# A two-layer trunk on one core: the first layer's experts in pairs with a side block, token lists by a product, the second filter spectrum moved

## The chip, the cores and the metric

One core of one Trainium2 chip runs the whole program. The metric is device time in microseconds, the median of the runs shown. All data and all arithmetic are float32. On TensorE every float32 product of this program stands in the trace as two MATMUL instructions and two weight loads, so "8 products" in the text are "x16" in a row.

## The reference, cut to what matters

Two layers work on 256 latent tokens and 256 context tokens, 1024 channels each. A layer has a part with four parallel token mixers and then a part with a mixture of experts. The second layer computes its last part for the latent tokens alone.

```python
def hier_moe(h, ...):                 # per token: best of 4 groups, then best 2 of that group's 4 experts
    gi = argmax(t @ w_rg + b_rg)      # group, weight gw = softmax at gi
    top_p, top_i = top_k(softmax(le[gi]), 2)
    ...
def expert_block(xblk, e):
    u = silu(xblk @ w1[e]) * (xblk @ w3[e])   # 1024 -> 512, twice
    return u @ w2[e]                          # 512 -> 1024
...
y = segment_sum(yb * buf_w[:, None], buf_tok) # each token gets its two weighted results
```

There are 16 experts. A token counts for two of them, so the first layer has 1024 assignments (64 per expert on average) and the second has 512 (32 on average). By the reference's own routing of these inputs the busiest expert has 86 assignments in the first layer (latent and context tokens together) and 48 in the second. One of the mixers (Hyena) convolves with a filter that a small network computes for each layer; the kernel brings it to the frequency domain with products (`fnorm`, `fdft`).

## The kernel before

**Order of the work.** `layer_order` writes one list of steps (engine, name) by hand, for TensorE (T), VectorE (V), ScalarE (S) and GpSimd (P). Each engine runs its own steps strictly in this order and waits on counting semaphores for the others. Steps of TensorE take the 8 PSUM banks in turn. On VectorE nearly every small instruction waits for the one before it (`link`). A second list (`CHUNKS`) sets the order in which SyncE's queue loads weights into a ring of three 2 MB places; a place is loaded again when its last reader has finished.

**Experts.** `xg` holds 128 gathered token rows; TensorE turns them (8 transposes, L1218 and L1125), VectorE and ScalarE copy them to `xgT`. Then come 8 products of 512 columns for the gate (`w1`), 8 for up (`w3`), 4 transposes of the hidden rows, and 4 + 4 products for down (`w2`). ScalarE and VectorE do the tanh form of silu between them, and ScalarE stores 128 result rows (512 KB) to `y_scratch`.
- First layer (not `paired`): 16 blocks of up to 128 rows, one expert each. Lines: gate L1229, up L1233, down L1249 and L1254, transposes L1218 and L1239. The weights of one expert are three 2 MB loads. The down products of expert e-1 stand behind gate and up of expert e.
- Second layer (`paired`): 8 blocks of two experts, 64 rows each. `both_halves` gives the even expert PSUM partitions 0 to 63 (L1130) and the odd one 64 to 127 (L1132), each with a stationary tile of 64 columns. The odd experts' weights lie in `n_` (w1), `hT` (w3) and `wide` (w2), so a pair takes six 2 MB loads: two behind each of gate, up and down of the pair before.
- If an expert has more assignments than its block has rows (`room`: 128, or 64 where paired), a branch runs more blocks, with every expert's weights loaded again.

**Routing.** From `lgout` (L2094) VectorE goes through route1 to route3 with two exponentials on ScalarE between them; ScalarE copies the transposed tokens (`hbout`, L1509) behind the second exponential and stores them to `h_scratch`. TensorE ranks the assignments (`rank`, L1104 to L1109), VectorE makes their places (`slots`), GpSimd scatters token numbers to a list in HBM (L1660; 8 DMAs in the first layer, 4 in the second), waits, reads the list back (L1665), copies an index and gathers the first block (L1674). While that goes on, VectorE runs the gate steps (`modgate`, L1832), and in the first layer TensorE, VectorE and ScalarE compute the second layer's filter spectrum (`fnorm` L930, `fnorms` L1925 to L1929, `fdft` L938 and L942, `fdftout` L1396 to L1403).

**Ahead of the routing** stands the last projection: 8 steps `wo` (L1076), their sums into `x` (L2086, L2088), squares (L1349), the scaled tokens `xn` (L1356 on ScalarE), and their transposes (`hT`, L878).

**Behind the experts** GpSimd waits for the last store of results and gathers each token's two rows (L1696, 8 DMAs in the first layer), ScalarE and VectorE weigh and add them, and the next layer begins.

## Time and profile before

| | |
|---|---|
| median of 3 runs (lowest to highest) | 1824.85 us (1823.38 to 1829.51) |
| profiled execution: its own time | 1827.23 us |
| its span in the trace | 1825.5 us |
| TensorE busy | 1553.3 us, 85% of the span |
| VectorE, ScalarE, GpSimd busy | 33%, 17%, 6% |
| mean TensorE clock granted | 0.924 of full speed |
| moved by DMA | 365.12 MB, mean 200 GB/s |
| first layer's experts, first gate product to last down product | 735.05 to 1100.06 us |
| second layer's experts, the same | 1558.19 to about 1802 us |

How to read it: the busy shares are averages over stages with different limits. The stage tables (busy time of each engine in a stretch, with clock and DMA rate) say what limits a stage; the timeline says which wait ends last in it. The clock column is the share of full speed; TensorE has two levels, 2.4 GHz (1.00) and 1.2 GHz.

### The profile page before, as it was taken

The page shows a single profiled execution, that of the slowest core. Times are in us where ns is not written, and L with a number is a line of the kernel's source. Part 1 is how long each engine was busy: PE and PEld are TensorE (multiplying, and loading weights), DVE is VectorE, ACT ScalarE, POOL GpSimd, SP SyncE. Part 2 cuts the span into 40 slices and gives each one's busy share as a digit, 9 for nine tenths or more (in the row PEclk, how much of TensorE's full clock was granted, in tenths as well). Part 3 has the DMA queues.
Part 4 walks back from the last instruction along what each step waited for, and adds up shares of the span by engine and source line. Part 5 has one row for each costly group of instructions (what it writes and reads, how often), then busy time and mean ns, then how long its engine had stood idle before and what let it go on. Part 6 is the DMA issues. An engine that isn't in the chain of part 4 may idle for free. (4 is left out here: it accounts for less than half of the span.)

```text
span 1825.5 us, 15949 instructions
## 1 busy us (share of the span) xinstructions
PE 1553.3 (85%) x5618; PEld 805.0 (44%) x5618; DVE 598.5 (33%) x1456; ACT 305.5 (17%) x611; POOL 115.6 (6%) x149
## 2 busy tenths in 40 slices
PE   5999998888999985999999982799979993887873
PEld 2444643433444444444444430655757862332321
DVE  4366443545432135111111102663555224010002
ACT  3112012221322112011111101211232201000000
POOL 0000000000111002000000001000001101000000
PEclk9999998999999997899999986899989996898997
DMA  9255021133111221588989857173212354799994
GB/s 381 108 231 218 35 92 69 47 138 116 46 67 53 92 92 50 225 329 335 337 333 338 331 193 311 46 283 131 94 74 111 116 220 172 281 431 426 428 427 190
DMA packets 34684, 365.12 MB, mean 200 GB/s; under 512 B 4256, under 2 KB 4656, under 8 KB 13888
## 3 DMA queue, kind: packets, MB, share of 16 engines
q1 hardware_dynamic: 24640, 329.67, 46.3%
q0 software_dynamic: 5664, 18.93, 2.7%
q10 hardware_dynamic: 4320, 15.73, 2.1%
q8 instruction: 36, 0.59, 0.1%
q14 instruction: 24, 0.20, 0.0%
HBM read 347.50 MB, written 16.82 MB: 200 GB/s over the span
## 5 line engine op out<-in xcount | busy, mean ns | idle before, releaser
L895 PE MATMUL ps<-hT,ring 128*128 128x512 f32 (+1 forms) x1344 | 460.5, 498 | 4.9 <-DVE hT L1858 3.2
L895 PEld LDWEIGHTS ps<-hT,ring 128*128 128x128 f32 x1344 | 258.7, 195 | 188.6 <-issue 160.8
L1130 PE MATMUL ps<-ring,m 128*64 128x512 f32 x384 | 186.8, 644 | 45.6 <-DMA n_<-w 19.7
L905 PE MATMUL ps<-ring,hT 128*128 128x512 f32 (+1 forms) x352 | 127.7, 522 | 2.5 <-DMA ring<-win 2.5
L1130 PEld LDWEIGHTS ps<-ring,m 128*64 128x64 f32 x384 | 54.9, 148 | 163.0 <-issue 140.7
L1229 PE MATMUL ps<-ring,m 128*128 128x512 f32 x256 | 115.5, 605 | 1.0 <-DVE m L2263 1.0
L1233 PE MATMUL ps<-ring,m 128*128 128x512 f32 x256 | 112.6, 593 | 0.3 <-DMA ring<-w 0.3
L993 PE MATMUL ps<-yT,ring 128*128 128x512 f32 (+1 forms) x256 | 94.5, 491 | 2.3 <-ACT n_ L1471 2.2
L905 PEld LDWEIGHTS ps<-ring,hT 128*128 128x128 f32 x352 | 67.0, 192 | 62.3 <-issue 58.1
L1076 PE MATMUL ps<-ring,wide 128*128 128x512 f32 x192 | 82.8, 593 | 0.8 <-POOL wide L1635 0.8
L1989 DVE SCALAR_TENSOR_TENSOR gtmp<-gth,ps 128x512 f32<-128x512 f32 (+1 forms) x48 | 26.6, 555 | 173.0 <-PE ps L993 149.5
L1430 ACT ACTIVATE gth<-ps,hbg 128x512 f32<-128x512 f32 (+1 forms) x64 | 37.1, 580 | 273.0 <-PE ps L895 212.7
L1233 PEld LDWEIGHTS ps<-ring,m 128*128 128x128 f32 x256 | 48.6, 190 | 61.9 <-issue 60.7
L1899 DVE SCALAR_TENSOR_TENSOR n_<-n_,col 128x512 f32<-128x512 f32 (+1 forms) x120 | 74.2, 618 | 4.3
L1229 PEld LDWEIGHTS ps<-ring,m 128*128 128x128 f32 x256 | 48.5, 194 | 56.9 <-issue 55.2
L1635 POOL TENSOR_TENSOR wide<-wide,gtmp 128x512 f32<-128x512 f32 (+1 forms) x48 | 47.9, 998 | 398.3 <-DVE gtmp L1989 398.3
L1132 PE MATMUL ps<-n_,m 128*64 128x512 f32 x128 | 69.2, 703 | 0.0
L1249 PE MATMUL ps<-ring,m 128*128 128x512 f32 x128 | 60.3, 616 | 8.2 <-issue 8.2
L2267 DVE SCALAR_TENSOR_TENSOR m<-m,ps 128x512 f32<-128x512 f32 x16 | 11.0, 687 | 166.6 <-ACT m L1575 166.6
L1132 PE MATMUL ps<-hT,m 128*64 128x512 f32 x128 | 61.6, 638 | 0.0
L854 PE MATMUL ps<-ring,cc 128*32 128x512 f32 x384 | 52.1, 665 | 10.7 <-DMA ring<-wmod 10.7
L1471 ACT ACTIVATE n_<-ps,nm 128x512 f32<-128x512 f32 (+1 forms) x72 | 43.9, 613 | 103.2 <-DVE nm L2031 56.0
(316 smaller groups left out, 1543.6 us busy)
## 6 DMA issues: line engine op xcount, KB each, us to landing
ring<-w SPq DMA_DIRECT2D x72, 2048.0 KB, 8.5
ring<-wmod SPq DMA_DIRECT2D x24, 2048.0 KB, 9.3
ring<-win SPq DMA_DIRECT2D x24, 2048.0 KB, 8.5
n_<-w SPq DMA_DIRECT2D x8, 2048.0 KB, 21.8
hT<-w SPq DMA_DIRECT2D x8, 2048.0 KB, 22.8
wide<-w SPq DMA_DIRECT2D x8, 2048.0 KB, 23.0
y_scratch<-m ACTq DMA_DIRECT2D x24, 512.0 KB, 8.5
ring<-wbr SPq DMA_DIRECT2D x8, 1024.0 KB, 4.8
```

What stands on the lines that cost most here:

```text
L854: last = pe.matmul(b[g:g + 32, :], cc[:, 32 * k:32 * k + 32], w[:, k, :], start=(k < 4), stop=(k >= 4), skip_group_check=True)
L895: last = pe.matmul(b[:, 0:W], w[:, k, jj * P:(jj + 1) * P], hT[:, k, 0:W], start=(k == 0), stop=(k == KD - 1))
L905: last = pe.matmul(b[:, 0:wid], hT[:, k, t * P:(t + 1) * P], w[:, k, 0:wid], start=(k == 0), stop=(k == KD - 1))
L993: last = pe.matmul(b[:, 0:W], w[:, k, j * P:(j + 1) * P], yT[:, bi in (1, 2), k, 0:W], start=(k == 0), stop=(k == 1))
L1076: last = pe.matmul(b, acc[:, k, t * P:(t + 1) * P], w[:, k, :], start=(k == 0), stop=(k == KD - 1))
L1130: pe.matmul(ps[0:HALF, bnk, :], left[:, k, 0:HALF], even[:, k, cols_], start=(k == 0), stop=(k == n_k - 1), skip_group_check=True)
L1132: last = pe.matmul(ps[HALF:P, bnk, :], left[:, k, HALF:P], odd[:, k, cols_], start=(k == 0), stop=(k == n_k - 1), skip_group_check=True)
L1229: last = pe.matmul(ps[:, 2, :], xgT[:, k, :], wg[:, k, :], start=(k == 0), stop=(k == KD - 1))
L1233: last = pe.matmul(ps[:, 3, :], xgT[:, k, :], wu[:, k, :], start=(k == 0), stop=(k == KD - 1))
L1249: last = pe.matmul(ps[:, 5, :], uT[:, f, :], wd[:, f, 0:512], start=(f == 0), stop=(f == 3))
L1635: last = nc.gpsimd.tensor_tensor(acc[:, j, 0:W], acc[:, j, 0:W], gtmp[:, g % 2, 0:W], ALU.add)
L1899: last = v.scalar_tensor_tensor(out=o, in0=ud[:, j, 0:ns, k:k + 256], scalar=w(k), in1=o, op0=ALU.mult, op1=ALU.add)
```

## The change

Three things, in all of both layers' routing and experts:

1. **Pairs in the first layer too, with a side block.** Every layer uses 8 blocks of two experts with 64 rows each. In the first layer (`with_side`) ranks 64 to 95 of each expert go to a side block: `side_x` has 64 rows, 32 for each expert of the pair. `four_quarters` runs products with stationary tiles of 32 columns on the four quarters of PSUM's partitions: for gate and up the quarters are (even, odd) by (lower, upper half of the 1024 channels), and VectorE adds the halves; for down they are (even, odd) by (lower, upper 512 outputs). A weight place is loaded again once the side block too has read it. `room` is 96 in the first layer and 64 in the second. TensorE's eight pairs are written out; the other engines write out the first and last pair and loop over the rest.
2. **Lists made on the chip.** The two exponentials go behind the list (`weights1`, `rexp`, `weights2`), `picks` holds the rest of the routing in fewer instructions. A product of one-hot ranks (`at_rank`) and token numbers (`token_of`) gives `lst` straight in PSUM; a second one gives the side block's list. The places of the results (`rows`) follow in VectorE's order, still ahead of its experts step. The scatter to HBM stays for the overflow branch alone. ScalarE copies the gates (`modgate`) of chunks 10 and 11.
3. **The second filter spectrum** moves from behind the routing to the last projection: `fnorm` and `fnorms` behind the first `wo` step, the four `fdft` behind the last, `fdftout` behind ScalarE's last square and ahead of its last `xn`.

```diff
 # layer_order
     for t in range(tt):
         for hf in range(2):
             o += [("T", ("wo", l, t, hf))]
+            if t == hf == 0 and spectrum:
+                o += spectrum[0]
...
             o += [("V", ("xup", l, t, hf))]
+    o += [g[0] for g in spectrum[1:]]
     o += [("S" if t % 2 else "V", ("xn", l, 2, t)) for t in range(tt - 1)]
-    o += norm_steps(l, 2, [tt - 1]) + modulated_steps(l, 2)
-    o += [("T", ("lg", l)), ("S", ("lgrow", l)), ("T", ("lgT", l)), ("V", ("lgout", l))]
-    o += [("V", ("route1", l)), ("S", ("rexp1", l)), ("V", ("route2", l)), ("S", ("rexp2", l)), ("V", ("route3", l))]
+    normed = norm_steps(l, 2, [tt - 1])
+    o += normed[:1] + [g[1] for g in spectrum[1:]] + normed[1:] + modulated_steps(l, 2)
+    o += [("T", ("lg", l)), ("S", ("lgrow", l)), ("T", ("lgT", l)), ("V", ("lgout", l)), ("V", ("picks", l))]
...
-    o += [("T", ("rank", l)), ("V", ("slots", l)), ("P", ("list", l))]
+    o += [("T", ("rank", l)), ("V", ("slots", l)), ("T", ("list", l)), ("V", ("list", l))]
+    if with_side(l):
+        o += [("V", ("sideslots", l)), ("T", ("sidelist", l)), ("V", ("sidelist", l))]
     o += gate_steps(l, (10, 11))
-    for g in spectrum:
-        o += g
+    o += [("V", ("weights1", l)), ("S", ("rexp", l)), ("V", ("weights2", l)), ("V", ("rows", l))]
     o += [("T", ("experts", l)), ("S", ("experts", l)), ("V", ("experts", l)), ("P", ("experts", l))]
 # SyncE, pairs 1 to 7
+                        for w in ("w1", "w3", "w2"):
+                            sp.wait_ge(last_reader(w, l), base + e)
+                            sp.dma_start(at[w][0], pairs_of[w][l, e, 0]).then_inc(at[w][1], 16)
+                            sp.dma_start(odd_at[w], pairs_of[w][l, e, 1]).then_inc(odd_landed[w], 16)
 # TensorE
+                elif kind == "list":
+                    for i, (q, t) in enumerate(choices):
+                        last = pe.matmul(b[:, 0:NE], at_rank[:, q * TILES + t, 0:P], token_of[:, q, t * NE:(t + 1) * NE],
+                                         start=(i == 0), stop=(i == len(choices) - 1))
...
+                    def four_quarters(bnk, left, quarters):
+                        for k in range(4):
+                            for g, (weights, k0, rows_, cols_) in enumerate(quarters):
+                                last = pe.matmul(ps[SIDE * g:SIDE * (g + 1), bnk, :], left[:, k0 + k, rows_:rows_ + SIDE],
+                                                 weights[:, k0 + k, cols_], start=(k == 0), stop=(k == 3),
+                                                 skip_group_check=True)
...
                     def gate_and_up(e):
...
                         both_halves(2, xgT, wg, wg2, slice(0, FE), KD).then_inc(gate_done, 1)
+                        if side:
+                            pe.wait_ge(side_xT_ready, e + 1)
...
+                            four_quarters(7, side_xT, split_k(wg, wg2)).then_inc(side_gate_done, 1)
                         both_halves(3, xgT, wu, wu2, slice(0, FE), KD).then_inc(up_done, 1)
+                        if side:
...
+                            four_quarters(6, side_xT, split_k(wu, wu2)).then_inc(side_up_done, 1)
...
+                    def pair(e, more):
+                        gate_and_up(e)
+                        if more:
+                            pe.wait_ge(tokens_gathered, e * 16 + 16 * (base + 2))
+                            turn_tokens()
+                        turn_u(e)
+                        if side and more:
+                            pe.wait_ge(side_gathered, e * 16 + 32)
+                            pe.wait_ge(side_gate_sum, e + 1)
+                            turn_side()
+                        down(e, more)
 # ScalarE, behind result(e)
+                        if side:
+                            act.wait_ge(side_y_ready, e + 1)
+                            act.dma_start(side_rows_of[e, :, 0:FE], side_y[0:HALF, :]).then_inc(side_y_stored, 16)
+                            act.dma_start(side_rows_of[e, :, FE:D], side_y[HALF:P, :]).then_inc(side_y_stored, 16)
 # GpSimd: no list step; the gathers take their index straight from lst
+                        gp.indirect_dma_start(out=xg, out_offset=None, in_=h2_dram,
+                                              in_offset=bass.IndirectOffsetOnAxis(ap=lst[:, e:e + 1], axis=0))\
+                          .then_inc(tokens_gathered, 16)
...
+                        gp.indirect_dma_start(out=side_x, out_offset=None, in_=h2_dram,
+                                              in_offset=bass.IndirectOffsetOnAxis(
+                                                  ap=lst[0:HALF, PAIRS + e:PAIRS + e + 1], axis=0))\
+                          .then_inc(side_gathered, 16)
 # VectorE
+                elif kind == "slots":
...
+                    link(v.tensor_scalar(ranks[:, 0:tt, :].rearrange("p t e -> p (t e)"), b[:, 0:tt * NE], 256.0, None, ALU.mult))
+                    link(v.tensor_tensor(pd, pk, ranks[:, 0:tt, :].unsqueeze(1).broadcast_to([P, 2, tt, NE]), ALU.mult))
+                    link(v.tensor_reduce(place_rank[:, :, 0:tt], pd, AX.X, ALU.add))
+                    last = one_hot_ranks(l, slice(0, P), 0, HALF)
```

In `down(e, more)` the side block's 4 transposes stand between the lower and the upper half, and its four quarters behind the upper half.

## Rows read from the trace of the kernel before

**Rows 1.** The page: its head, and a VectorE group (count, busy, mean ns).
```profile
span 1825.5 us, 15949 instructions
...
L1899 DVE SCALAR_TENSOR_TENSOR n_<-n_,col 128x512 f32<-128x512 f32 (+1 forms) x120 | 74.2, 618 | 4.3
```

**Rows 2.** Stages: first layer's experts; 32 us of the second's.
```profile
core 0: us, PE busy (x) PEld busy (x) DVE busy (x) ACT busy (x) POOL busy (x), PEclk, DMA share, GB/s
735.00:1100.00 365.00, 356.34 (x952) 166.56 (x952) 43.44 (x63) 37.02 (x62) 17.04 (x29) 0.98 0.81 302
...
1603.00:1635.00 32.00, 25.35 (x117) 9.78 (x115) 3.70 (x6) 3.30 (x6) 1.33 (x3) 0.95 1.00 427
```

**Rows 3.** Timeline, TensorE, first layer's experts: start us, us, what, count.
```profile
735.05 9.90 PE L1229 MATMUL ps<-ring,m 128*128 128x512 f32 x16 [0.85 <-DVE m L2263]
...
1060.93 7.03 PE L1229 MATMUL ps<-ring,m 128*128 128x512 f32 x16
...
1067.80 7.03 PE L1233 MATMUL ps<-ring,m 128*128 128x512 f32 x16
...
1096.46 3.60 PE L1254 MATMUL ps<-ring,m 128*128 128x512 f32 x8
```

**Rows 4.** Timeline, TensorE, second layer: a pair's last up products to its first down.
```profile
1573.62 0.59 PE L1130 MATMUL ps<-ring,m 128*64 128x512 f32 x1
1573.62 0.59 PE L1132 MATMUL ps<-hT,m 128*64 128x512 f32 x1
1574.05 0.59 PE L1130 MATMUL ps<-ring,m 128*64 128x512 f32 x1
...
1574.58 1.09 PE L1125 MATMUL ps<-con,m 128*128 128x128 f32 x8
...
1575.51 0.66 PE L1151 MATMUL ps<-con,m 128*128 128x128 f32 x4
...
1577.04 0.61 PE L1130 MATMUL ps<-ring,m 128*64 128x512 f32 x1 [0.87 <-ACT m L1543]
```

**Rows 5.** Timeline, TensorE: one modulation step, 8 products on four partition quarters.
```profile
1115.02 1.92 PE L854 MATMUL ps<-ring,cc 128*32 128x512 f32 x16
```

**Rows 6.** Timeline, first layer's routing, from lgout to the turned first block.
```profile
692.44 0.24 DVE L2094 TENSOR_TENSOR m<-m,row 128x80 f32<-128x80 f32 x1
...
703.10 0.69 PE L1104 MATMUL ps<-m,con 128*128 128x80 f32 x2 [7.80 <-DVE m L2151]
...
705.60 0.17 DVE L2192 CAST m<-con 128x4 uint32<-128x4 f32 x1 [2.64 <-PE ps L1109]
...
711.88 0.17 DVE L2213 CAST m<-m 128x16 uint32<-128x16 f32 x1
...
712.95 1.04 POOL L1660 DMA_INDIRECT list_scratch<-m  x1 [94.55 <-issue]
...
727.93 1.01 POOL L1674 DMA_INDIRECT m<-h_scratch,m  x1 [0.52 <-POOL m L1672]
...
732.26 1.94 PE L1218 MATMUL ps<-con,m 128*128 128x128 f32 x8 [6.25 <-DMA m<-h_scratch,m]
```

**Rows 7.** Timeline, second layer: end of lgout, and the first gate product.
```profile
1522.15 0.20 DVE L2094 TENSOR_TENSOR m<-m,row 128x40 f32<-128x40 f32 x1
...
1558.19 1.11 PE L1130 MATMUL ps<-ring,m 128*64 128x512 f32 x1 [1.11 <-DVE m L2221]
```

**Rows 8.** Timeline: the filter spectrum, and TensorE's wait behind the last projection.
```profile
680.75 1.52 PE L878 MATMUL ps<-con,wide 128*128 128x128 f32 x6 [6.78 <-ACT wide L1356]
...
708.70 3.41 PE L930 MATMUL ps<-con,m 128*128 128x1 f32 x16
...
724.38 0.38 ACT L1399 ACTIVATE m<-ps 128x256 f32<-128x256 f32 x1 [0.40 <-PE ps L938]
```

**Rows 9.** Timeline, end of the first layer: last store of results, first gather of them.
```profile
1100.72 0.35 ACTq L1586 DMA_DIRECT2D y_scratch<-m  x1
...
1114.10 0.94 POOL L1696 DMA_INDIRECT wide<-y_scratch,m  x1 [80.12 <-ACTq L1612]
```

More of the change, by code:

```diff
@@ L36 @@
 HALF = P // 2
+SIDE = HALF // 2
 FE = 512
@@ L430, in readers @@
            "yM": ("V", "yrA"), "yR": ("V", "ynA"), "yC": ("S", "yToutC"),
-           "wo": ("V", "xup"), "lg": ("S", "lgrow"), "lgT": ("V", "lgout"), "hb": ("S", "hbout"), "rank": ("V", "slots")}
+           "wo": ("V", "xup"), "lg": ("S", "lgrow"), "lgT": ("V", "lgout"), "hb": ("S", "hbout"), "rank": ("V", "list"),
+           "list": ("V", "list"), "sidelist": ("V", "sidelist")}
     if kind in one:
@@ L434, in readers @@
         return [(e, (k, l, *rest))]
+    if kind == "modB":
+        return [(spreader(rest[0]), ("modgate", l, *rest))]
     if kind == "yA":
@@ L1152, in turn_u, with turn_side_u, down @@
                         last.then_inc(u_turned, 1)
-                    def down(e):
+                    def turn_side_u(e):
+                        pe.wait_ge(side_u_ready, e + 1)
+                        for f in range(4):
+                            last = pe.transpose(ps[:, 2, f * HALF:(f + 1) * HALF], side_u[:, f * P:(f + 1) * P],
+                                                ident[0:HALF, 0:HALF])
+                        last.then_inc(side_u_turned, 1)
+                    def down(e, more):
@@ L1176, in _ @@
+                    for e in range(PAIRS):
+                        pair(e, e < PAIRS - 1)
                     pe.wait_ge(y_low, base + PAIRS)
                     pe.wait_ge(y_high, base + PAIRS)
+                    if side:
+                        pe.wait_ge(side_y_ready, PAIRS)
                     count = assignments(pe, l)
-                    with pe.If(count > HALF):
+                    with pe.If(count > room(l)):
                         with pe.Fori(0, more_blocks(l) * NE) as n_block:
@@ L1676, in _ @@
-                    with gp.Fori(1, blocks(l)) as e:
-                        gp.wait_ge(tokens_turned, base + e)
-                        gp.tensor_copy(idx1, lst[:, bass.ds(e, 1)]).then_inc(index_ready, 1)
-                        gp.wait_ge(index_ready, base + e + 1)
-                        gp.sem_inc(waited, 1)
+                    gp.wait_ge(vector_done, vector("list", l))
+                    for e in range(PAIRS):
+                        if e:
+                            gp.wait_ge(tokens_turned, base + e)
@@ L2153, in _ @@
                     last.then_inc(vector_done, 1)
-                elif kind == "slots" and paired(l):
+                elif kind == "slots":
+                    pk = pick[:, :, 0:tt * NE].rearrange("p q (t e) -> p q t e", e=NE)
+                    for q in range(2):
+                        last = v.tensor_tensor(token_of[:, q, 0:tt * NE].rearrange("p (t e) -> p t e", e=NE), pk[:, q],
+                                               c("token")[:, 0:tt].unsqueeze(2).broadcast_to([P, tt, NE]), ALU.mult)
+                    link(last)
@@ new lines, in _ @@
+                    link(v.tensor_tensor(pd, pk, c("expert").unsqueeze(1).unsqueeze(1).broadcast_to([P, 2, tt, NE]), ALU.mult))
+                    link(v.tensor_reduce(ex, pd, AX.X, ALU.add))
+                    slot, ry = slotf[:, 0:2, 0:tt], slotf[:, 2:4, 0:tt]
+                    link(v.scalar_tensor_tensor(out=slot, in0=rk, scalar=float(NE), in1=ex, op0=ALU.mult, op1=ALU.add))
+                    link(v.tensor_scalar(slot, slot, float(MORE_AT - NE * room(l)), None, ALU.add))
+                    link(v.scalar_tensor_tensor(out=ry, in0=ex, scalar=float(HALF), in1=rk, op0=ALU.mult, op1=ALU.add))
@@ new lines, in _ @@
+                    per_expert, at = HALF, 0
+                    ends = [(HALF, SIDE, SIDE_AT - HALF)] if with_side(l) else []
+                    for end, rows_, start in ends + [(room(l), P, MORE_AT - room(l))]:
+                        link(v.tensor_scalar(st, ex, float(rows_ - per_expert), float(start - at), ALU.mult, ALU.add))
+                        link(v.tensor_scalar(mo, rk, float(end), None, ALU.is_ge))
+                        link(v.tensor_tensor(st, st, mo, ALU.mult))
+                        link(v.tensor_tensor(ry, ry, st, ALU.add))
+                        per_expert, at = rows_, start
@@ new lines, in pair @@
+                    def pair(e, more):
+                        activated(e)
+                        if side:
+                            side_activated(e)
+                        hidden(e)
+                        if side:
+                            side_hidden(e)
+                        if more:
+                            turned(e + 1)
+                        if side and more:
+                            side_turned_out(e + 1)
+                        result(e)
+                        if side:
+                            side_result(e)
```

729 lines of the change are left out of this document (299 added, 430 removed).

## The prediction

> **What bounds the kernel now.** I read the page first: TensorE is busy 85% of the 1825.5 us span [rows 1], so a stage table comes next. In it the first layer's experts take 365 us, a fifth of the span, with TensorE busy 356 of them at a clock of 0.98 and DMA at 302 GB/s: TensorE is the bound there. A stretch of the second layer's experts shows the opposite: DMA share 1.00 at 427 GB/s, TensorE busy 25 of 32 us [rows 2]. The timeline gives the unit: 8 products of 512 columns take 1067.80 - 1060.93 = 6.87 us, 0.859 each, at 2.4 GHz; the first eight cost 9.90 instead of 7.03, since TensorE had idled and stood at 1.2 GHz [rows 3]. In the second layer the two halves start in the same instant and the next two 0.43 us later: two products of 64 columns side by side cost what one of 128 does [rows 4]. Between last layer step and experts lies the routing: 692.44 to 735.05 us in the first layer, and in it TensorE waits for VectorE, then for a list's way through HBM [rows 6]. The second layer's is 1522.15 to 1558.19 [rows 7].
>
> **First layer's experts.** Before: 735.05 to 1096.46 + 3.60 = 1100.06, so 365.0 us [rows 3], 16 times 20.6 us of products and small things. After, one pair's TensorE time:
> - gate, up, down: 24 product pairs x 0.859 = 20.6 us;
> - side block: 48 products of 32 columns in 12 groups of four. The modulation step is the same form (8 products on four quarters, each quarter its own moving data): 1.92 us with its tail, four steps of 0.43 [rows 5]. So 12 x 0.859 = 10.3 us. Bounds: nothing below; above 41 us if the quarters went one by one;
> - from the last up product to the first down product 1577.04 - 1574.48 = 2.6 us with 12 transposes and a wait for the copy of the turned hidden rows [rows 4]. The side block's 8 transposes (0.9 us at the price of full ones [rows 4], half that if their 64 rows count) fall into that wait. Its other 4 cost 0.5, and I add 0.4 for semaphores: 3.5 us.
>
> Together 34.4 us. The silu of the side block (ScalarE two copies and a tanh, VectorE two sums and two products, each 0.6 to 0.7 us by 512-column instructions such as [rows 1]) is needed only behind the lower down half, over 6 us after the side up products, and both engines are busy under 45 of 365 us there [rows 2]: hidden. Should it come late, what waits next is `turn_side_u`, and behind it the upper down half.
>
> DMA per pair: six loads of 2.10 MB, gather and store of 128 rows (0.52 MB each), and 0.26 + 0.26 MB for the side: 14.2 MB, at 427 GB/s [rows 2] 33.1 us. That is under 34.4, but close. w1 is asked for behind the side gate (at 10.3 us of the pair) and needed at 34.4; w3 at 20.6, needed 24 us later; w2 at 34, needed 23 us later. 4.2 MB take 9.8 us, so each has over 10 us to spare and TensorE sets the pace.
>
> Eight pairs: 7 x 34.4 + a last one without the next tokens' transposes, 33.0, + 2.9 for the slow start [rows 3] = 276.7 us. **Gain 88.3.** The first pair's odd w1 is asked for before the routing, odd w3 behind the `hb` transposes, odd w2 behind the stores to `h_scratch`; each needs 5 to 10 us and all are there before the first gate product.
>
> **First layer's routing.** Link by link, a small VectorE instruction costs 0.217 us: `slots` has 30 from 705.60 to 711.88 [rows 6]. I count from the end of lgout, 692.68.
> - picks: 21 dependent instructions, 4.5 us (route1 to route3 took 10.4 with their two exponentials) -> 697.2
> - rank: 703.10 to 705.60 = 2.5 [rows 6] -> 699.7
> - slots: three small ones 0.9 and two one-hot tables of 512 columns (0.62 each by [rows 1]) -> 702.0
> - list: 8 products of few columns, 3.4 by the 8 of L930 [rows 8] -> 705.4; copies 0.7 -> 706.1
> - sideslots (two tables of 256) 0.9, sidelist 3.4 -> 710.4
> - then TensorE's four modB, the last ends 3.6 later, ScalarE's modgate 0.6, rexp 0.5, weights2 1.2 -> 716.4
> - rows: 23 instructions, 4.9 -> 721.3; the copies of the turned tokens 1.2 -> first gate product 722.7.
>
> GpSimd's gather starts near 706.4 and needs 4.3 us as before (727.93 to 732.26 [rows 6]); the side's lands near 715.5. So VectorE's `rows` is what ends last: the new wait in the old one's place. Before it was 735.05. **Gain 12.3.** Queued behind `rows` on VectorE is only its own experts step, for which TensorE waits.
>
> **The moved spectrum.** Behind the routing it stood beside the scatter and cost nothing, so nothing is won there. In its new place fnorm (16 MATMULs of few columns, 3.41 us in [rows 8], about 3.1 at 2.4 GHz) lengthens the projection, which TensorE fills. fdft, about 4.3 us, goes into the 6.78 us that TensorE waits for the last scaled tile [rows 8]. But ScalarE now makes seven copies of 0.38 [rows 8] between its last square and the last xn: 3.3 us beside the 2.7 for which it waited for VectorE, 0.7 late. fnorms on VectorE (some 3.8 us) lies beside products. **Loss 3.8.** Without that cover fdft would cost 4.3 more.
>
> **Behind the first layer's experts** the last store was issued at 1100.72 and the gather began at 1114.10, 13.4 us for 512 KB beside three fresh weight loads [rows 9]. Now the large store leaves 2.7 us ahead of those loads, since they wait for the side block; the side's 256 KB leave 1 us behind. Bounds: 2 us lost (one more copy, two more issues), 8 won. I take 3 won.
>
> **Second layer.** No side block. The same count from the end of lgout, 1522.35: picks 4.3, rank 1.6, slots 1.6, list of 4 products 1.8, copies 0.6 -> 1532.3; gather 4.6 -> 1536.9; 8 slow transposes 1.9 as in [rows 6] -> 1538.8. Beside it modB, modgate, rexp, weights2 and the 15 instructions of `rows` end at 1539.1. First gate product near 1540.2 instead of 1558.19 [rows 7]: **gain 18.0.** The loop is bound by DMA, but each of its loads is asked for by a product of the pair before, so the whole stream moves up; the loop itself and the end stay as they are. TensorE's written-out pairs cost nothing here: it has 6.6 us to spare in 32 [rows 2].
>
> **Sum.** -88.3 - 12.3 + 3.8 - 3 - 18.0 = -117.8 us against the profiled execution's own 1827.23 (span 1825.5 [rows 1] and 1.7 around it): 1709.4. The median of the runs lies 2.4 lower, so I forecast **1707 us**. A measurement of this kernel can tell about 0.3%, 5.5 us, from no change.
>
> **Rivals.**
> - *DMA sets the pace of the pairs.* For it: 33.1 against 34.4, side rows stored in 2 KB pieces, small gathers. Against: 427 GB/s already holds gathers and stores. At 36 us a pair, and a slower clock at each wait as in the second layer (0.95 [rows 2]): +13, 1720 us. 0.16.
> - *Four quarters are worth only three*: one product of each four finds no room beside the others, a group costs 4/3 of 0.859 us, a pair gains 12 x 0.286 = 3.4 and the whole 27: 1734 us. Rows 5 speak against it: 8 products in 1.92 us. 0.11. The Trainium skill, TensorE: Matmul & The Clock Gate, section "Measured speedup vs the span model", has 3.07 measured for four row tiles; by that figure a group costs 4/3.07 and the sum would be 25 us longer. The trace does not agree with it for column tiles of this form.
> - *The quarters share in twos*, since here the moving data comes from two tiles in turn and the stationary data is new for each product: +10.3 a pair, 1789 us. 0.03.
> - *The other side: the quarters run one after another*, as four products of full cost (PSUM banks 6 and 7 written by both kinds of tile, drained in between). 48 x 0.859 in place of 10.3 is +30.9 a pair, 247 in all: 1954 us, slower. It decides from 14.7 us extra a pair, 25 us for the side products. Against it: rows 5. 0.03.
> - *The change doesn't do what it says:* an expert has over 96 assignments, so the overflow branch runs 4 x 16 blocks of some 40 us (14.7 of loads, 20.6 of products, copies, store): about 4250 us. The routing of the reference gives 86. 0.01.
>
> **How the numbers follow.** Forecast case 0.66; its own range is 1693 to 1722 (a pair 33.4 to 36, routing 4 us either way, stores +2 to -8). To leave out no more than 2 in 10 the range takes in the first two rivals: 1693 to 1737. Faster 0.96, same 0.01, slower 0.03; within 0.3% only a partly serial side block ends.
>
> **What would show it.** In the profile after: pairs 34.4 us apart in the first layer and a clock near 1.00; side products starting in fours; DMA share near 0.95; first gate product about 30 us behind lgout, and released by VectorE, not by a DMA; TensorE's wait ahead of L878 nearly gone; the second layer's stage table as before. Wrong it would be if TensorE's waits in the pairs name DMA (first rival), if side groups are spaced over 0.43 us per MATMUL (second to fourth), or if a wait for the gather still ends last in the routing.

## The result, and the profile after it

The changed kernel takes 1714.3 us (median of 4 runs, 1711.12 to 1716.12) against 1827.18 for the kernel before; the ratio is 0.938, 95% interval 0.936 to 0.941. Forecast were 1707 us and a range of 1693 to 1737. The profiled execution took 1713.2 us with a span of 1711.5, against 1827.2 and 1825.5 [rows 1]: 114.0 us less, where the terms of the forecast summed to 117.8.

Page of the changed kernel: its head, then a TensorE group of the pairs (busy us, mean ns of one | idle before, releaser).

```profile
span 1711.5 us, 17194 instructions
...
L1138 PE MATMUL ps<-ring,m 128*64 128x512 f32 x768 | 358.4, 620 | 47.6 <-DMA n_<-w 21.1
```

Stages of the changed kernel, as in [rows 2]: the first layer's experts, then 32 us of the second's.

```profile
core 0: us, PE busy (x) PEld busy (x) DVE busy (x) ACT busy (x) POOL busy (x), PEclk, DMA share, GB/s
721.97:998.59 276.62, 275.17 (x1713) 90.95 (x1712) 54.97 (x86) 32.31 (x55) 12.20 (x14) 1.00 0.89 361
1489.00:1521.00 32.00, 25.26 (x108) 9.63 (x108) 2.76 (x4) 2.28 (x4) 0.98 (x2) 0.89 1.01 429
```

365.0 us of experts have become 276.6, TensorE busy for 275.2 of them at full clock. The second layer's experts still wait for DMA at 429 GB/s. The span, stretch by stretch (us):

| stretch | before | after | forecast change | measured |
|---|---|---|---|---|
| first layer's experts | 365.0 | 276.6 | -88.3 | -88.4 |
| first routing, end of lgout to first gate product | 42.4 | 28.0 | -12.3 | -14.3 |
| first product of the last projection to end of lgout (the moved spectrum) | 73.8 | 74.9 | +3.8 | +1.1 |
| last expert product to the next layer's first transposes | 52.0 | 52.5 | -3 | +0.5 |
| second routing | 35.8 | 23.9 | -18.0 | -11.9 |

These sum to -113.0; the last 1.0 lies in stretches that the change does not touch. The three parts of the change were not all tried alone (only the moved spectrum was, below): what each is worth is read from its own stretch. The term that was off by most is the second routing. Timeline of the changed kernel, second layer, from the end of lgout to the first gate product (start us, us, engine, line, what, [idle before <- releaser]):

```profile
1420.18 0.20 DVE L2038 TENSOR_TENSOR m<-m,row 128x40 f32<-128x40 f32 x1
...
1421.68 0.33 SPq L761 DMA_DIRECT2D hT<-w  x1
...
1423.51 0.33 ACTq L1474 DMA_DIRECT2D h_scratch<-wide  x1
...
1429.33 0.16 DVE L2090 CAST m<-ps 64x8 uint32<-64x8 f32 x1 [2.12 <-PE ps L1098]
...
1432.18 0.33 SPq L763 DMA_DIRECT2D wide<-w  x1
...
1432.91 0.97 POOL L1594 DMA_INDIRECT m<-h_scratch,m  x1 [55.26 <-DMA h_scratch<-wide]
...
1441.50 1.94 PE L1127 MATMUL ps<-con,m 128*128 128x128 f32 x8 [10.50 <-DMA m<-h_scratch,m]
...
1444.28 1.12 PE L1138 MATMUL ps<-ring,m 128*64 128x512 f32 x1 [0.84 <-DVE m L2154]
```

The list begins to be copied at 1429.33, 8.95 us behind the end of lgout, where the forecast's count had 9.3. But GpSimd's gather starts only at 1432.91, released by the token stores, of which the last was issued 9.4 us earlier, beside a 2 MB load into `hT` (the odd expert's w3). And the gather itself takes 8.6 us beside the next 2 MB load (into `wide`, w2). In the kernel before, second layer, neither stood on the path:

```profile
1525.13 0.33 SPq L736 DMA_DIRECT2D hT<-w  x1
...
1529.74 0.35 ACTq L1516 DMA_DIRECT2D h_scratch<-wide  x1
```

There ScalarE's copies stood behind the second exponential, so the stores left 4.6 us behind the load of w3 and landed in 3.8 us (median), where they now leave together with it and take 9.0. And the load of w2 left at 1535.11 and had landed long before the gather at 1550.86, since GpSimd's scatter and its way back, from 1538.76 on, stood between them. Three places to test follow: these two loads, what bounds the pairs, and the stores behind the first layer's experts.

### The profile page after: what moved, and what is told of

Its sections match the earlier page's. It is cut to its first block and busy times, and to the rows that moved or that the text cites. A ratio compares the mean times of both kernels' runs of the same rounds, so it can differ in the third digit from the quotient of the medians.

```text
span 1711.5 us, 17194 instructions
## 1 busy us (share of the span) xinstructions
PE 1471.4 (86%) x6426; PEld 731.5 (43%) x6426; DVE 604.8 (35%) x1458; ACT 303.8 (18%) x609; POOL 97.3 (6%) x111
## 5 line engine op out<-in xcount | busy, mean ns | idle before, releaser
L1138 PE MATMUL ps<-ring,m 128*64 128x512 f32 x768 | 358.4, 620 | 47.6 <-DMA n_<-w 21.1
L1138 PEld LDWEIGHTS ps<-ring,m 128*64 128x64 f32 x768 | 104.8, 142 | 269.9 <-issue 254.8
L1140 PE MATMUL ps<-n_,m 128*64 128x512 f32 x256 | 126.1, 650 | 0.0
L1140 PE MATMUL ps<-wide,m 128*64 128x512 f32 x256 | 116.6, 604 | 0.0
L1140 PE MATMUL ps<-hT,m 128*64 128x512 f32 x256 | 116.6, 609 | 0.0
L975 PEld LDWEIGHTS ps<-yT,ring 128*128 128x128 f32 x256 | 45.6, 190 | 31.8 <-issue 23.7
L1148 PE MATMUL ps<-ring,yT 128*32 128x512 f32 x256 | 58.1, 595 | 0.0
L1058 PEld LDWEIGHTS ps<-ring,wide 128*128 128x128 f32 x192 | 36.3, 190 | 45.5 <-issue 45.5
L1011 PE MATMUL ps<-con,n_ 128*128 128x128 f32 x160 | 28.6, 302 | 31.2 <-DVE n_ L1998 20.3
## 6 DMA issues: line engine op xcount, KB each, us to landing
ring<-w SPq DMA_DIRECT2D x48, 2048.0 KB, 10.5
```

The costliest lines, as they stand in the source:

```text
L975: last = pe.matmul(b[:, 0:W], w[:, k, j * P:(j + 1) * P], yT[:, bi in (1, 2), k, 0:W], start=(k == 0), stop=(k == 1))
L1058: last = pe.matmul(b, acc[:, k, t * P:(t + 1) * P], w[:, k, :], start=(k == 0), stop=(k == KD - 1))
L1138: pe.matmul(ps[0:HALF, bnk, :], left[:, k, 0:HALF], even[:, k, cols_], start=(k == 0), stop=(k == n_k - 1), skip_group_check=True)
L1140: last = pe.matmul(ps[HALF:P, bnk, :], left[:, k, HALF:P], odd[:, k, cols_], start=(k == 0), stop=(k == n_k - 1), skip_group_check=True)
L1148: last = pe.matmul(ps[SIDE * g:SIDE * (g + 1), bnk, :], left[:, k0 + k, rows_:rows_ + SIDE], weights[:, k0 + k, cols_], start=(k == 0), st ...
```

## The experiments

All kernels are the changed one with the edit shown, except spectrum_only. Routing times below run from the end of lgout to the first gate product; "transposes" is the time from the start of the last upper down product of the first layer's experts to the next layer's first transposes.

| kernel | median us | 1st routing | 2nd routing | transposes |
|---|---|---|---|---|
| changed | 1714.30 | 28.0 | 23.9 | 56.7 |
| the same again | 1714.86 | 28.0 | 24.5 | 56.3 |
| hold_w2 | 1708.79 | 27.2 | 19.8 | 56.0 |
| hold_both | 1705.91 | 27.3 | 17.6 | 56.2 |
| hold_rexp | 1704.23 | 23.8 | 18.8 | 56.6 |
| hold_next | 1714.69 | 27.4 | 24.8 | 56.9 |
| best3 | 1695.17 | 23.8 | 18.6 | 46.1 |
| best4 | 1685.65 | 23.8 | 18.2 | 40.3 |

### The two odd loads held until the first gathers have landed

```diff
-sp.wait_ge(tensor_done, tensor("hb", l, live(l) - 1, 1))
-sp.dma_start(odd_at["w3"], w3[l, 1])...
 sp.wait_ge(h2_stored, 16 * (live(l) + l * live(0)))
+sp.wait_ge(tokens_gathered, 16 * (base + 1))
+if with_side(l):
+    sp.wait_ge(side_gathered, 16)
+sp.dma_start(odd_at["w3"], w3[l, 1])...
 sp.dma_start(odd_at["w2"], w2[l, 1])...
```

> The changed kernel with one edit: the loads of the odd expert's second and third matrices (w3, w2) for each layer's first pair wait until the first token gathers have landed. Theory (the 2 MB loads stretch the token stores and the gather): in the second layer the stretch from the router's last sum to the first gate product falls from 23.9 to about 18 us, in the first layer from 28.0 to 27 to 28 (the row numbers on VectorE end next there), the experts behind are unchanged; time about 1708 us, ratio to the kernel before 0.935. Rival (the stores and the gather take that long by themselves, so the forecast of 4.6 us was simply too small for them): both stretches unchanged, 1714. Second rival (the held loads come too late for the first up and down products): the first gate product comes 6 us earlier but the first pair is longer by 3 to 6 us, 1711 to 1714.

Measured: 1705.91 us (1701.97 to 1707.46), ratio 0.933 (0.931 to 0.936). The second routing takes 17.6 us, what the first theory said (and the forecast: 17.8). Timeline of hold_both, second layer:

```profile
1418.49 0.20 DVE L2040 TENSOR_TENSOR m<-m,row 128x40 f32<-128x40 f32 x1
...
1428.97 0.97 POOL L1596 DMA_INDIRECT m<-h_scratch,m  x1 [53.01 <-DVE m L2107]
...
1433.46 1.94 PE L1129 MATMUL ps<-con,m 128*128 128x128 f32 x8 [4.14 <-DMA m<-h_scratch,m]
...
1436.24 1.11 PE L1140 MATMUL ps<-ring,m 128*64 128x512 f32 x1 [0.84 <-DVE m L2156]
```

The gather is no longer released by the stores but by VectorE's list, and is done 4.5 us later instead of 8.6.

With w2 alone held the two costs come apart (hold_w2: the waits for the gathers stand ahead of w2's load, and w3's lines stay where they were):

> The changed kernel with one edit: only the odd expert's third matrix (w2) of each layer's first pair waits for the first token gathers; w3 goes out beside the token stores as it does now. If stores and gather each pay for the load beside them: the gather takes about 5 us instead of 8 to 9, the last store still some 8.5 us; second layer's stretch about 20.5 us, time about 1711. If only the load beside the stores matters: stretch 23.9, 1714. If only the one beside the gather matters: as with both held, about 18 us and 1708.

Measured: 1708.79 us, ratio 0.936 (0.934 to 0.938); second routing 19.8. Timeline of hold_w2, second layer:

```profile
1432.41 0.97 POOL L1597 DMA_INDIRECT m<-h_scratch,m  x1 [55.20 <-DMA h_scratch<-wide]
...
1436.96 1.94 PE L1130 MATMUL ps<-con,m 128*128 128x128 f32 x8 [6.41 <-DMA m<-h_scratch,m]
```

The gather starts as late as before (12.5 us behind lgout in both, 10.3 with both held) and then takes 4.6 us. So of 6.3 us the load beside the gather cost 4.0 and the one beside the stores 2.2. Both were on the path.

The first routing barely moved, 28.0 to 27.3: there the turned tokens came only 0.7 us behind VectorE's rows. Timeline of the changed kernel, first layer:

```profile
719.05 1.94 PE L1127 MATMUL ps<-con,m 128*128 128x128 f32 x8 [5.58 <-DMA m<-h_scratch,m]
...
721.10 0.69 DVE L2154 COPY m<-ps 128x512 f32<-128x512 f32 x1 [0.70 <-PE ps L1127]
```

And that 0.7 was given back in the first pair. Stage windows of the changed kernel, then of hold_both, from the first gate product on:

```profile
721.97:726.00 4.03, 4.03 (x17) 1.37 (x18) 0.69 (x1) 0.00 (x0) 1.14 (x2) 0.79 0.64 192
726.00:730.00 4.00, 4.00 (x24) 1.14 (x22) 0.00 (x0) 0.08 (x1) 0.00 (x0) 1.00 0.02 7
```

```profile
719.91:724.00 4.09, 4.09 (x10) 1.24 (x12) 0.54 (x1) 0.00 (x0) 0.00 (x0) 0.50 1.02 430
724.00:728.00 4.00, 4.00 (x18) 1.19 (x16) 0.00 (x0) 0.00 (x0) 0.00 (x0) 0.78 0.76 253
```

The clock stands behind the five engines' busy times; from there to the first reload of w1 it is 1.00 in both. Both kernels reload w1 at 733.66 by their own time, though hold_both began 2.06 us sooner (0.7 by its routing, the rest by a drift of the stages ahead of it). With its tokens turned early, TensorE had idled 5.4 us before the first gate product:

```profile
719.91 1.12 PE L1140 MATMUL ps<-ring,m 128*64 128x512 f32 x1 [5.38 <-DVE m L2156]
```

It ran at 0.50, 1.2 GHz, for all of the first window and, by the mean of 0.78, for 1.8 us of the second: 5.9 us. In the changed kernel the turning of both token blocks ran up to the gate, and by its mean of 0.79 the slow part lasted 1.7 us. The difference of 4.2 us at half speed is the 2.06 us. None of TensorE's waits in that first pair names a DMA, so the second rival of the expectation (weights too late) is not what happened.

That the idle time made the slow part longer is not shown. hold_rexp and best3 (both below) have the same order in this routing and the same wait of 1.86 us ahead of the first gate product. Their first windows:

```profile
718.39:722.39 4.00, 4.00 (x14) 1.29 (x16) 0.54 (x1) 0.00 (x0) 0.00 (x0) 0.66 0.97 406
```

```profile
718.27:722.27 4.00, 4.00 (x10) 1.23 (x12) 0.54 (x1) 0.00 (x0) 0.00 (x0) 0.50 1.00 420
```

The slow part lasted 2.7 us in hold_rexp and, with a mean of 0.75 in the next 4 us, 6.0 in best3. From the first gate product to the first reload of w1 the runs take 11.7 or 11.8 us (changed kernel, twice), 12.2 (hold_rexp) or 13.8 to 13.9 (hold_both, hold_w2, best3, best4). So 2 us can go or stay here with nothing different in the order, and what decides it is open. The 8.4 us between the medians of the changed kernel and hold_both are likewise more than the routings explain (7.0), and the first pair takes 2.1 of those back; the rest lies in stages that the edit does not touch.

### What sets the pace of the pairs

side_short leaves out three quarters of the side block's products, small_loads half the bytes of each first-layer load from the second pair on, short_small both. Each ran once.

```diff
 def four_quarters(...):                                  # side_short
-    for k in range(4):
+    for k in range(1):
...
+n = WCH // 2 if l == 0 else WCH                          # small_loads
-sp.dma_start(odd_at[w], pairs_of[w][l, e, 1])...
+sp.dma_start(odd_at[w][:, 0:n], pairs_of[w][l, e, 1][:, 0:n])...
```

(the even load in small_loads likewise)

> The changed kernel with three quarters of the side block's products left out (each group of four quarters runs its first of four steps alone, in gate, up and down): TensorE has 3 x 3 x 0.86 = 7.8 us less to do in each pair of the first layer's experts, all loads as before. Theory (TensorE sets the pair's period of 34.6 us, the transfers lie just under it): the period falls, but only to the transfers' own time, 33.1 to 34.4 us for 14.1 MB at 427 to 410 GB/s, and waits on DMA appear on TensorE; time 1702 to 1713. Rival (TensorE alone binds, the transfers have slack because they merely queue early): period about 27 us, time about 1654.

> The changed kernel with half of the bytes of each expert weight load left out in the first layer from the second pair on (the other half of each buffer keeps the first pair's weights): the transfers of a pair fall from 14.1 MB to about 7.8. Theory (TensorE sets the period): the period stays at 34.4 to 34.6 us, time within 3 us of 1714. Rival (the transfers set it, TensorE's 34.9 of 35 us busy being the time that it is stretched to): the period falls towards 27 to 30 us, time below 1690.

> Both cuts together on the changed kernel: three quarters of the side block's products and, from the second pair on, half of the bytes of the first layer's expert loads left out. Theory (with the products cut alone the period fell only to 34.2 us because the transfers take that long): now it falls to TensorE's own work, 34.6 - 7.8 = 26.8 us, or about 28.5 if the engine's busy time of that run is its need at the lower clock it had; time 1650 to 1665. Rival (a wait between the engines, not the transfers, set the 34.2): the period stays above 31 us, time above 1685.

Measured: 1695.24 us for side_short, 1712.14 for small_loads, 1653.07 for both cuts. The period is read from the reloads of w1 on the SP queue: 34.57 us in the changed kernel and in small_loads, 34.24 in side_short (791.02 to 927.98 in four pairs), 26.85 with both cuts (787.04 to 894.43 in four). Stage windows, 3 or 4 pairs each: changed kernel, small_loads, side_short, short_small.

```profile
792.00:895.00 103.00, 102.70 (x644) 34.53 (x648) 21.07 (x33) 12.30 (x21) 5.53 (x6) 1.00 1.01 412
```

```profile
791.00:894.50 103.50, 103.20 (x652) 34.61 (x648) 21.06 (x33) 12.30 (x21) 5.53 (x6) 1.00 0.62 229
```

```profile
790.50:927.50 137.00, 114.33 (x576) 42.39 (x576) 28.11 (x45) 16.44 (x29) 7.38 (x8) 0.95 1.01 412
```

```profile
787.04:894.43 107.39, 106.99 (x578) 36.78 (x576) 28.09 (x45) 16.40 (x28) 7.40 (x8) 1.00 0.81 294
```

TensorE's waits in side_short, 760 to 960 us (us in total, times, longest):

```profile
PE ps L1138 <- DMA n_<-w: 17.7, 6, 4.0
PE ps L1138 <- DMA hT<-w: 11.9, 5, 2.5
...
```

In the changed kernel the same view has no row at all. With half the bytes the period does not move by 0.01 us: TensorE sets it. With less work for TensorE it falls by 0.3 us only and TensorE waits for weights: the transfers come next, 34.24 us for 14.1 MB at 412 GB/s. With both cuts it is 26.85, which excludes a wait between the engines. From pair to pair the stage is balanced to 1%, so there fewer bytes alone bring nothing and less work for TensorE alone 0.3 us a pair. Of the 18 us by which side_short's span is shorter, 16.5 still lie in the stage, 14.3 of them in its first and last pairs, whose weights are already there. The other 1.6 stand ahead of the stage, where the edit changes nothing.

The runs also price a group of four quarters: 34.57 - 26.85 = 7.72 us for nine groups left out, 0.858 each, against 0.859 for one full product [rows 3]. Four products of 32 columns cost what one of 128 does, and they start together. Timeline of the changed kernel, one row of each group:

```profile
994.95 0.62 PE L1148 MATMUL ps<-ring,gth 128*32 128x512 f32 x1
...
995.40 0.59 PE L1148 MATMUL ps<-ring,gth 128*32 128x512 f32 x1
```

The Trainium skill (TensorE: Matmul & The Clock Gate, section "Measured speedup vs the span model") measures 3.07 for four row tiles. For four column tiles of this form the runs show 4.0, so that figure does not carry over to them.

### The row numbers ahead of the gate copies

hold_rexp is hold_both with one more edit:

```diff
-o += gate_steps(l, (10, 11))
 o += [("V", ("weights1", l)), ("S", ("rexp", l)), ("V", ("weights2", l)), ("V", ("rows", l))]
+o += gate_steps(l, (10, 11))
```

> The kernel with both loads held (hold_both), and one more edit: the routing's softmax weights and row numbers on ScalarE and VectorE are queued ahead of the eight gate transposes' copies instead of behind them. Theory (with the loads held, VectorE's row numbers are what ends last in the first layer, 4.0 us of them a wait for ScalarE's exponentials behind four copies): the first layer's stretch from the router's last sum to the first gate product falls from 27.3 to 23.3 us, the second layer's stays at 17 to 18 (there the gather ends last, rows end 0.7 us before the tokens are turned); time 1702. Rival (the tokens, not the rows, end last in both): no change, 1706. Second rival (the copies of the gates come late and hold TensorE's banks, which the turning of the tokens needs): the stretch falls by 1 us or less.

Measured: 1704.23 us (1698.48 to 1706.38), ratio 0.931 (0.930 to 0.933). The first routing falls to 23.8 us, 3.5 less. VectorE's wait in the changed kernel, then in hold_rexp:

```profile
714.60 0.17 DVE L2111 TENSOR_REDUCE m<-m 128x4 f32<-128x16 f32 x1 [4.02 <-ACT m L1460]
```

```profile
711.65 0.17 DVE L2113 TENSOR_REDUCE m<-m 128x4 f32<-128x16 f32 x1 [0.51 <-ACT m L1462]
```

The theory holds for the stage. In the total it is 1.7 us, inside the spread: the second routing was 1.2 us longer in this profile (its gather took 5.1 us instead of 4.5, in best4 too; why is open).

### The spectrum moved, alone, on the kernel before

The edit is the part of the change that touches `spectrum` in `layer_order`, with the rest of the kernel before.

> The kernel before with the one part of the change that moves the second filter's spectrum behind the last projection; routing, lists and experts as before. The forecast's term: +3.8 us, time 1831, ratio 1.002. Theory from the trace after the change: +1.3 us, 1828.5, ratio 1.0007, seen in the stretch from the last update of x to the router's last sum (2.0 us longer up to the first transposes, 0.7 shorter behind them) and no change behind it, since where it stood it ran beside the wait for the list. Rival (its old place cost time, because its products and ScalarE's copies stood ahead of the first gate product): faster than before by 1 us or more.

Measured: 1828.19 us (12 runs) against 1828.18 (17 runs), ratio 1.0003 (0.9992 to 1.0013). Counted from the first product of the last projection, so that the drift of earlier stages drops out, the end of lgout comes at 695.85 - 620.93 = 74.9 us instead of 692.68 - 618.87 = 73.8. Timeline of spectrum_only:

```profile
620.93 7.03 PE L1077 MATMUL ps<-ring,wide 128*128 128x512 f32 x16
627.80 1.84 PE L931 MATMUL ps<-con,m 128*128 128x1 f32 x16
...
684.65 5.35 PE L879 MATMUL ps<-con,wide 128*128 128x128 f32 x32 [2.20 <-ACT wide L1357]
...
695.61 0.24 DVE L2095 TENSOR_TENSOR m<-m,row 128x80 f32<-128x80 f32 x1
```

So the move costs 1.1 us there, the same in the full change (74.9), and wins nothing behind: first gate product 117.1 us after that start instead of 116.2. `fnorm` costs 1.84 us and not 3.1: right behind the projection's products, at a granted clock of 1.00, its sixteen MATMULs take 0.115 us each; in its old place (3.41 us [rows 8]) the clock was 0.50. The wait ahead of the transposes shrank from 6.78 [rows 8] to 2.20, and the transposes got shorter, 6.26 to 5.35, at a mean clock of 0.68 instead of 0.58. By the total alone the move is within the noise, and harmless.

### The loads of the next layer

```diff
+if not held and CHUNK_AT.get(("w2", 0), 0) < i:           # hold_next
+    held.append(i)
+    sp.wait_ge(y_stored, 16 * PAIRS)
+    sp.wait_ge(side_y_stored, 32 * PAIRS)
 src = source[name[0]][name[1], name[2]]
```

> The changed kernel with one edit: the next layer's first loads (five, 9 MB) wait until the first layer's experts' outputs have been stored. Theory (the three 2 MB loads issued as the last products end stretch the two 128 KB stores of the side block to 12 us): the gather of the outputs starts at 3 to 5 us behind the last product instead of 15.2, and the stretch until the first tile is weighed falls from 29.6 us by about 8; the loads then run beside the gathers. Time about 1706, ratio 0.934. Rival (the loads are needed early: the next layer's modulation products wait for them and ScalarE's copies of those stand ahead of the weighing): first tile no earlier, time 1714 or up to 5 us more.

Measured: 1714.69 us (1710.27 to 1716.65), ratio 0.938 (0.936 to 0.939): nothing won. Timeline of the changed kernel behind the last products, then of hold_next:

```profile
999.38 0.51 ACTq L1519 DMA_DIRECT2D y_scratch<-gth  x1
999.53 17.98 SPq L794 DMA_DIRECT2D ring<-win  x3
999.92 0.68 ACTq L1520 DMA_DIRECT2D y_scratch<-gth  x1
...
1013.75 0.94 POOL L1620 DMA_INDIRECT wide<-y_scratch,m  x1 [93.40 <-PE ps L842]
...
1028.24 1.15 ACT L1547 ACTIVATE wide<-wide,m 128x1024 f32<-128x1024 f32 x1 [10.39 <-DMA hT<-y_scratch,m]
```

```profile
1003.38 0.82 SPq L799 DMA_DIRECT2D ring<-wmod  x2
...
1005.17 0.94 POOL L1625 DMA_INDIRECT wide<-y_scratch,m  x1 [83.82 <-issue]
...
1022.98 1.15 ACT L1552 ACTIVATE wide<-wide,m 128x1024 f32<-128x1024 f32 x1 [1.13 <-DMA hT<-y_scratch,m]
...
1032.96 1.15 ACT L1552 ACTIVATE wide<-wide,m 128x1024 f32<-128x1024 f32 x1 [8.84 <-DMA hT<-y_scratch,m]
```

The mechanism is as stated: the side's two stores, 128 KB each, took 10.5 us (median) beside the loads, while the 512 KB store ahead of the loads landed in 2.6; in hold_next, where the two were issued at 1000.38 and 1000.89, SP saw them landed at 1003.38. The gathers begin 5.6 us behind the last product instead of 15.2. But the gain was then lost to the next collision: the eight gathers of 512 KB now ran beside the same 9 MB and took 24.7 us each (median), the first tile came 10 us ahead of the second, and the transposes stood where they were (56.9). So holding the loads a little only moves the contention from the stores to the gathers. They have to stay back until the gathers are through.

### Together

best3 is hold_rexp, the wait above put on `y_gathered` of all four tiles, and the two modulation products of chunks 4 and 5 queued behind the norm.

> All together on the changed kernel: the first pair's two odd loads held until the first gathers have landed, softmax and rows ahead of the gate copies, and the next layer's first loads held until all outputs of the first layer's experts have been gathered, with the two modulation products that need them queued behind the norm's steps instead of ahead of the weighing. Theory: 12 us in the two routings (11.9 to 18 us and 28.0 to 23.3), and behind the first layer's experts gathers that start 3 to 5 us after the last product and land four tiles in 12 us, so that the next layer's first transposes start about 20 us sooner; the first input projection then has its weights just in time. Time about 1682, ratio 0.920. Rival (the loads come too late for the next layer's first products): the transposes start 20 us sooner and the projections wait for DMA 5 to 12 us, 1690. Rival (contention was not what stretched the stores and the gathers): 1702.

Measured: 1695.17 us (1694.11 to 1696.02), ratio 0.927 (0.926 to 0.929). The transposes came 10.6 us sooner, not 20. The weighing of the first tile began 17.2 us sooner, counted from the last upper down product, but TensorE's order had both modulation products ahead of the transposes, the second one behind a copy that ScalarE made only after the norm. best4 mends that order:

```diff
-o = norm_steps(l, 1, range(TILES)) + [s for c in (4, 5) for s in mod_steps(l, [c])]
+squares, normed = norm_steps(l, 1, range(TILES))[:TILES], norm_steps(l, 1, range(TILES))[TILES:]
+m4, m5 = mod_steps(l, [4]), mod_steps(l, [5])
+o = squares + m4[:1] + m5[:1] + m4[1:3] + normed + m5[1:3] + m4[3:] + m5[3:]
 o += modulated_steps(l, 1) + pads
...
-for t in range(TILES):
+for t in range(TILES - 1):
     sp.wait_ge(y_gathered[t], 32)
```

> best3 with its order behind the first layer's experts mended: the next layer's loads wait for three of the four output tiles instead of four, both modulation products stand together on TensorE, and ScalarE copies the first one's row ahead of the last scalings of the norm instead of behind them. Theory (in best3 the next layer's first transposes had their inputs at 1032.2 us but stood behind the second modulation product, which stood behind a copy queued on ScalarE, until 1038.96): they start 5 to 6 us sooner, nothing else moves; time about 1689.5, ratio 0.924. Rival (the first input projection then waits for its weights, whose loads start 2 us sooner at most): 2 us or less are gained, 1693.

> The changed kernel itself, unedited, on the same chip and against the same runs as best4, since single runs of every kernel here spread over 4 to 9 us. Expected 1714 us, ratio 0.938, by every theory; the stretches 28.0 and 23.9 us in the two routings again, if they are the waits' work and not chance; should the second one come out at 20 or less, what the held loads gained there was chance.

Measured: best4 1685.65 us (1683.24 to 1689.39), ratio 0.923 (0.921 to 0.925); the changed kernel again 1714.86 (1713.02 to 1715.2), ratio 0.938 (0.937 to 0.940). Timeline of best4:

```profile
1003.80 0.94 POOL L1629 DMA_INDIRECT wide<-y_scratch,m  x1 [83.82 <-issue]
...
1010.39 1.15 ACT L1556 ACTIVATE wide<-wide,m 128x1024 f32<-128x1024 f32 x1 [15.11 <-DMA hT<-y_scratch,m]
...
1016.36 0.82 SPq L803 DMA_DIRECT2D ring<-wmod  x2
...
1034.34 3.66 PE L869 MATMUL ps<-con,wide 128*128 128x128 f32 x32
...
1080.70 7.10 PE L896 MATMUL ps<-ring,hT 128*128 128x512 f32 x16 [1.82 <-DMA ring<-win]
```

With the loads held, the eight gathers take some 6 us each (median). The transposes start 5.8 us sooner than in best3, as expected, and they take 3.66 us at a clock of 1.00 (in best3 too), where the changed kernel's took 5.46 at 0.67: there TensorE had been idle before them, here products stand just ahead. "Nothing else moves" did not hold: the way from there to the second layer's lgout is 4.2 us shorter than in best3. It begins at the input projection, whose eight products with the next load waited 3.9 us for DMA in best3 and then took 9.86 us at a mean clock of 0.72; here they wait 1.82 and take 7.10 at 1.00. That wait is shorter than the changed kernel's at the same place, 3.0. best4's two edits (the order, and three tiles instead of four) were not tried apart. best4 beats the changed kernel by 29 us and the kernel before by 142.

## Why the prediction was right, and where it was off

The time, the sign and the range held, and the term that makes three quarters of the gain was right by its own steps. Four smaller terms were mis-sized, and that the sum came within 4 us of the span's change is in part luck: two errors (2.0 and 2.7 us) went the good way, two (6.1 and 3.5) the other.

- **First layer's experts, -88.3: right** (-88.4), by its own steps. Pairs are 34.57 us apart, forecast 34.4; the clock is 1.00; the side products start in fours 0.43 us apart. The rivals of three quarters, of twos and of one after another fall with the 0.858 us that a group of four costs.
- **The first rival, DMA as the pace,** was nearer than the text had it. It took the 427 GB/s of the second layer as the rate; here 412 are moved at a share of 1.01, so the transfers need 34.24 us and not 33.1. TensorE wins by 0.3 us. "DMA share near 0.95" was wrong for the same reason.
- **First routing, -12.3: 2.0 more.** The chain was right link by link but for the side's list: eight products with 64 stationary columns take 1.86 us, where the count had 3.4, the price of 128 columns. "VectorE's `rows` is what ends last" was wrong by a little: rows ended at 720.40, and then VectorE idled 0.70 us for the tokens, turned from 719.05 to 720.99. The gather had started at 709.28 and landed 9.8 us later, where the count had 706.4 and 4.3; rows all but hid that. So the text's own sign of being wrong, a wait for the gather that still ends last, came in both layers. hold_rexp shows what was in the rows: a 4 us wait for ScalarE behind four gate copies, which the text counted but did not call avoidable.
- **Second routing, -18.0: the step that failed** is "gather 4.6 -> 1536.9", with the sentence that the odd loads "all are there before the first gate product". They were; but the question was whom they would delay. The stores held the gather back by 2.2 us and the gather took 4.0 longer. Without the two loads the stage takes 17.6 us where the text said 17.8. In the kernel before, the second exponential had kept the stores behind the load of w3, and the scatter the gather behind the load of w2.
- **Moved spectrum, +3.8: mis-sized, +1.1.** fnorm costs 1.84 and not 3.1: the text took 3.41 us as nearly the full-speed price, though it was measured at a clock of 0.50. And the term left out that the transposes behind run faster, by almost 1 us. TensorE's wait ahead of them fell to 2.2 us, not to nearly nothing.
- **Behind the first layer's experts, -3: mis-sized, +0.5.** The large store left ahead of the loads as said. But the two small ones "1 us behind" were taken to land soon; they stood beside the loads and took 10.5 us. The bound "2 us lost" was the one to take.
- **Second layer's experts and the end, 0: right.** The stretch is 0.1 us shorter. Whether TensorE's pairs, written out, cost or win anything against a loop was not tried by itself.

## What to carry to other kernels

When a long serial wait is removed, list every transfer that used to run inside it, and ask of each not whether it lands in time but what small transfer it now stands beside: here two early 2 MB loads cost 6 us of a routing by stretching 512 KB stores and gathers, and TensorE did not wait for them when they were held back. Holding a load pays only if it is held past every short transfer on the path; held past the first alone, the loss moves to the next. And compare the granted clock at the start of a stage before crediting an earlier start: here the first pair gave back some 2 us, in some runs and not in others.

## What was not expected of the hardware

- A transfer of 128 to 512 KB beside 2 MB loads takes two to five times as long: 512 KB stores 9.0 us (median) instead of 2.6, 128 KB stores 10.5 instead of 2.3, a 512 KB gather 8.6 instead of 4.5. Whether it waits behind their bytes or is served slowly among them was not separated.
- At a DMA share of 1.00 or 1.01, 427 to 429 GB/s are moved in the second layer's experts and 412 in the first's. That the side block's small transfers make the difference is likely but not tested; small_loads points the same way, with 229 GB/s at a share of 0.62 (369 for a full share), but there the loads' rows are shorter too.
- A product of few moving columns costs by its stationary columns and by the clock: at a granted clock of 0.50, 0.45 us with 128 (3.57 for 8) and 0.23 with 64 (1.86 for 8); at 1.00, 0.23 with 128 (1.84 for 8, fnorm).
- How long the first gate products ran at 1.2 GHz differed between runs: 1.7 us in the changed kernel, 5.9 in hold_both, but also 2.7 in hold_rexp and 6.0 in best3, with the same order and the same 1.86 us of idle before. It is worth some 2 us a stage and was not explained.
